# ScalarE makes a slot's coefficient ahead of its share of the mixer's work

## The reference

```
def peer_ffn(h, w_q, sub_keys, u, v):          # in chunks of 128 tokens
    q = (xc @ w_q).reshape(128, 8, 2, 128)
    s = einsum('thpd,pnd->thpn', q, sub_keys)
    sv, si = top_k(s, 16)                      # per half
    top_s, pos = top_k(sums of all 16 x 16 pairs, 16)
    idx = the experts at pos
    g = softmax(top_s)
    act = gelu(einsum('td,thkd->thk', xc, u[idx]))
    return einsum('thk,thkd->td', g * act, v[idx])
```

## Time and profile before

| | |
|---|---|
| median of 3 runs | 2242.47 us (2241.41 to 2242.71) |
| the profiled execution | 2243.3 us, span 2241.5 us |
| granted PE clock, mean | 0.979 |
| PE busy | 2026.6 us (90%) |
| DVE busy | 1587.6 us (71%) |
| ACT busy | 1111.0 us (50%) |
| POOL busy | 622.2 us (28%) |
| gather: 512 indirect DMAs | first issued at 810.5 us, last at 2213.1 us |

### The profile page before, as it was taken

The page is one execution under the profiler, slowest core; times in us unless marked ns, Lnnn a source line. Parts: engine busy times, 40 slices in busy tenths (PEclk is TensorE's granted clock), DMA queues, the critical chain, the costliest instruction groups (busy, mean ns, idle before and its releaser), DMA issues.

```text
span 2241.5 us, 28545 instructions
## 1 busy us (share of the span) xinstructions
PE 2026.6 (90%) x9926; PEld 1299.9 (58%) x9926; DVE 1587.6 (71%) x3688; ACT 1111.0 (50%) x2704; POOL 622.2 (28%) x612
## 2 busy tenths in 40 slices
PE   8899999999999988887789979998999999888876
PEld 7789999789999975432234434443444443333322
DVE  7857778768788888666676486567567656776654
ACT  5456436466534455454444475444356544444543
POOL 0000011100011024344433343344234344444442
PEclk9899999999999999999999999999999999999999
DMA  6225698726598579999999999999999999999996
GB/s 236 77 94 203 222 339 294 248 84 213 195 357 301 186 276 413 421 421 421 422 421 412 421 416 421 405 421 411 420 419 392 421 421 422 421 422 421 421 421 289
DMA packets 130773, 764.58 MB, mean 341 GB/s; under 512 B 14416, under 2 KB 16208, under 8 KB 59088
## 3 DMA queue, kind: packets, MB, share of 16 engines
q0 software_dynamic: 87552, 587.24, 64.1%
q1 hardware_dynamic: 42368, 174.15, 21.6%
q10 hardware_dynamic: 720, 1.51, 0.2%
HBM read 761.80 MB, written 1.05 MB: 340 GB/s over the span
## 4 chain that ended last, share of the span: by engine, by line
PE 52%; DMA 30%; DVE 10%; ACT 4%; issue 3%; POOL 1%; DVEq 0%; POOLq 0%; ACTq 0%
DMA arena<-experts,arena 28%; PE bank L1082 15%; PE bank L589 9%; PE bank L591 9%; PE bank L590 9%; PE bank L1118 7%; DVE arena L2664 3%; DMA alibi<-ada_w 1%; POOL arena L560 1%; DVE wlo L1969 1%; ACT arena L1696 1%; PE bank L773 1%; ACT arena L1480 1%; ACT arena L1695 1%; DMA arena<-ada_w 1%
## 5 line engine op out<-in xcount | busy, mean ns | idle before, releaser
L1082 PE MATMUL bank<-arena 128*128 128x512 f32 x2048 | 979.2, 617 | 154.3 <-ACT arena L1696 153.8
L2664 DVE CUSTOM_DVE_ANT_0 arena<-arena 128x1024 f32<-128x1024 f32 x512 | 626.1, 1224 | 444.6 <-DMA arena<-experts,arena 443.8
L560 POOL DMA_INDIRECT arena<-experts,arena x512 | 570.8, 1115 | 928.8 <-PE bank L1082 792.0
L1082 PEld LDWEIGHTS bank<-arena 128*128 128x128 f32 x2048 | 375.3, 194 | 708.9 <-issue 364.5
L1691 ACT ACTIVATE arena<-arena 128x1 f32<-128x1 f32 x512 | 103.3, 202 | 563.5 <-DVE arena L2664 561.5
L1367 ACT CAST whi<-wring 128x1024 fp32r<-128x1024 f32 x229 | 239.2, 1050 | 226.7 <-PE bank L591 221.4
L1969 DVE TENSOR_TENSOR wlo<-wring,whi 128x1024 fp32r<-128x1024 f32 x229 | 279.0, 1223 | 73.3 <-ACT whi L1367 72.6
L1696 ACT ACTIVATE arena<-tab,arena 128x128 f32<-128x128 f32 x512 | 205.6, 401 | 16.7
L549 POOL DMA_DIRECT2D arena<-ada_w x64 | 34.2, 535 | 571.0 <-DVE adaM L2016 558.0
L589 PE MATMUL bank<-hTh,whi 128*128 128x256 f32 (+1 forms) x584 | 170.5, 292 | 1.9 <-DVE wlo L1969 1.4
L591 PE MATMUL bank<-hTh,wlo 128*128 128x256 f32 (+1 forms) x584 | 165.4, 283 | 0.0
(11 more groups left out here) (403 smaller groups left out, 2897.1 us busy)
## 6 DMA issues: line engine op xcount, KB each, us to landing
wring<-w_stream SPq DMA_DIRECT2D x233, 512.0 KB, 4.3
wring<-w_stream SPq DMA_DIRECT2D x46, 1024.0 KB
arena<-ada_w POOLq DMA_DIRECT2D x64, 512.0 KB, 5.5
alibi<-ada_w POOLq DMA_DIRECT2D x32, 512.0 KB, 5.5
arena<-experts,arena POOLq DMA_INDIRECT x512
xT<-xT_in SPq DMA_DIRECT2D x2, 544.0 KB, 4.2
alibi<-alibi_in ACTq DMA_DIRECT2D x1, 1024.0 KB, 5.3
tab<-tab_in SPq DMA_DIRECT2D x1, 847.0 KB, 10.6
```

What stands on the lines that cost most here:

```text
L560: pool.indirect_dma_start(g_ring[:, r], None, experts[n // (2 * PEER_HEADS)], bass.IndirectOffsetOnAxis(idx[:, s // SLOTS % 2, s % SLOTS:s ...
L1082: last = mm(banks[2 * t + b][:, :], diag[:, r], g_ring[:, r, D + b * TILE_N:D + (b + 1) * TILE_N], start=s % SLOTS == 0, stop=s % SLOTS == ...
L2664: v.tensor_tensor_reduce(g_ring[:, r, 0:D], g_ring[:, r, 0:D], hrow[:, t], 1.0, 0.0, ALU.mult, ALU.add, act8[:, r:r + 1]).then_inc(dot_don ...
```

## The change

In ACT's loop over the slots behind the early ones (slots 0 to 59 are done in an earlier loop, without parts), the call of coefficient(s) goes from behind the parts that begin at slot s to ahead of them:

```
             beside = [None, mixer_parts(0), mixer_parts(1), last_parts(0)]
             for s in range(early, N_SLOTS):
+                coefficient(s)
                 for _ in range(parts_begun(s)):
                     next(beside[s // SLOTS])
-                coefficient(s)
             last_rows()
```

## The result

The changed kernel takes 2247.87 us (median of 20 runs, 2244.39 to 2251.88) against 2243.05 for the kernel before in the same comparison (20 runs, 2240.88 to 2245.58). The ratio is 1.0020, 95% interval 1.0014 to 1.0026: **4.8 us slower**. The forecast was 2254, 11.5 slower. The direction was right and the time lies inside the range; the size was over twice too large, and a size is what the working claimed to give. The *no change* rival had 2242 to 2247, whose upper end is nearer to the result than the forecast is. The profiled execution has a span of 2246.3 us, against 2241.5.

What follows compares the result with a forecast made beforehand. DMA at its 421 to 422 GB/s ceiling was taken as the bound, with 9.5 us of empty transfer time to regain. 2243.3 + 2.3 + 1.0 + 5 + 3 = 2254.6, less 0.83 for the median: 2254 us; range 2241 to 2265.

Steps and rivals of the forecast that it cites:

- no change: Rival: the ring covers both tiles' delays but for the copies of (a), or less; 2242 to 2247 us, chance 0.21.
- (a): copy_f at slot 3 of each mixer: PE's transposes start 2.27 us later; +2.3 us at tile 1, +1.0 at tile 0.
- (b) tile 0's pairs: Softmax pairs of tile 0's mixer: shorter operations, fuller queue, last dot 6.4 us late; +3 us of empty DMA time.
- (b) tile 1's pairs: Softmax pairs at slots 36, 40, 43, 47: Exp load comes onto the path, DVE's stream late; +5 us of empty DMA time.
- (c): Norm parts: square root later, coefficient earlier, opposing edits; oT copies later but transfers full behind them; 0 us.
- (d): Parts waiting for PE (row copy L1736): coefficient no longer behind that wait, PE has diagonals in hand; 0 us.
- The walk through the pairs: Tile 1's four pairs, step by step: joins 2.1, 4.1, 7.3 us late, fourth adds 3.7, slot 48's dot 7.6 late.
- the allowance for cover: Behind tile 1's pairs: queue covers about two late gathers; +5 us taken, against 7.6 if nothing is covered.
- Faster: Rival: PE's wait for the diagonal after the exponentials is the path, so the change gains; 2237 us, chance 0.08.
- Much slower: Rival: parts' results lie behind the slot's gather, PE keeps a slot less of the ring; 2273 us, chance 0.09.
- The forecast's own test: Forecast is wrong if DVE's new waits appear without GB/s below 402 in 1600 to 1700 and 419 in 1300 to 1400.
- The drain: Skill's 1.38 us per table switch at eight Exp loads: estimate 11 us, time near 2265; given no chance of its own.

Runs made afterwards that it cites:

- copies: Kernel before with the coefficient ahead of the part only at slot 3 of each tile (131, 259, 387): 2242.48 against 2242.44 us, ratio 0.9999.
- pairs_tile0: Kernel before with the coefficient ahead only at the four pair slots of tile 0's mixer: 2242.54 against 2242.44 us, ratio 1.0000.
- pairs_tile1: Kernel before with the coefficient ahead only at slots 36, 40, 43, 47 of tile 1's mixer: 2246.87 against 2242.44 us, ratio 1.0018.
- rest: Kernel before with the coefficient ahead on all slots but both mixers' pair slots and slot 3 of each tile: 2244.08 against 2242.44 us, ratio 1.0006.
- dot_first: Kernel before with ACT's coefficient and DVE's dot both ahead of the part at both mixers' pair slots: 2242.91 against 2243.06 us, ratio 1.0000.
- dve_long_tile1: Kernel before with 44 chained memsets on DVE ahead of slot 48 of tile 1's mixer: 2244.86 against 2243.18 us, ratio 1.0010.
- the four pieces: The change split into pairs_tile1, pairs_tile0, copies and rest, each applied alone to the kernel before; ratios 1.0018, 1.0000, 0.9999 and 1.0006.

## Why the prediction was right in direction and wrong in size

**The bound** was right. Transfers run at 421 or 422 GB/s while experts are gathered, before and after, and PE's waits for L1696 (98.3 us from 1140 to 2230 us before, 100.5 after) aren't what is paid: copies has 104.6 at no measured cost.

**The step that failed is the sum**: "2243.3 + 2.3 + 1.0 + 5 + 3". Three of its four terms, 6.3 of 11.3 us, were priced where they arise and not where they end. "DMA already runs dry there, so all of it counts" is the sentence that is wrong: what the copies lost at 1550 us came back at the pairs, up to 1720 us. The measured worth of the four terms:

- (a) both copies, forecast 3.3: PE's wait grew by 2.3 at each place as worked out, the time by 0.0 (copies, interval -2.2 to +1.8 us).
- (b) tile 0's pairs, forecast 3: the lag of 3.8 us at slot 48 came, with a dip of 2.4 us in the change, and went; 0.1 (pairs_tile0, interval -2.0 to +2.0).
- (b) tile 1's pairs, forecast 5: 4.4 (pairs_tile1), and 5.4 in the changed kernel's profile. This term was about right.
- (c), (d), forecast 0: 1.6 (rest), interval -0.7 to +3.4; not told from 0.

The reason could be read in the dips of the earlier trace rows: transfers wait there for the engines, so a shortfall ahead of a dip can be made up in it. Behind tile 1's pairs there is hardly any. For tile 0's pairs and for tile 1's copies the return stands outside the spread of the profiles; for tile 0's copies only the time says so. The prediction used this for the gain (no more than the empty time can be had) and not for the loss.

**The walk through the pairs** had the mechanism right: coefficient, Exp load, exponentials, join, and DVE's stream as what stays late (dot_first shows that the order of dot, masks and load is the cause; that a late stream alone is paid there has only dve_long_tile1's 1.7 us, 0.2 to 4.3, for it). Its lags were 2.1, 4.1 and 7.3 us at the joins and 7.6 at slot 48; measured are 1.5, 2.7, 5.1 and 4.5. The join waits for its own head's two exponentials and not for all four, 0.98 us per pair less. The +5 was right partly by luck: the allowance for cover was too large by about as much as the lag.

**The rivals.** Faster: out; the interval lies above 1. Much slower: out; the piece that holds the row copies costs 3.4 us at most. No change: two of the four pieces cost nothing and a third can't be told from it, so as a mechanism the rival was right for tile 0's pairs and for the copies, and wrong for tile 1's pairs. The forecast's own test held: DVE's new waits are there (seven, up to 3.0 us) and GB/s is lower in 1300 to 1400. But 407 against 419 is a weak sign, since the six kernels that leave tile 0 alone have 409 to 421 there, and 1600 to 1700 rose from 402 to 408; its loss came in the next window, 398 against 422. The drain that the Trainium skill counts in a table switch ("ScalarE: Activation LUTs", What ACT_TABLE_LOAD costs) shows in no row here: the exponential starts at 1682.39, 0.01 us behind the load.

## What to carry to other kernels

Price a loss at the point from which nothing gives it back. With a ring in front of a saturated DMA queue, list the dips of before, from more than one execution: here a delay with dips behind it cost nothing (tile 0's pairs, 0.1 us), and the same edit behind the last of them cost 4.4 us. When an operation is moved ahead of another on one engine, ask for each whether what it waits for, and its table load, ran in the shade of a wait before: here the coefficient came in front at no measured cost once DVE made its dot in front as well.

## What the runs showed of the hardware

In these traces a table load runs ahead of the wait of its activation, so that an engine that waits long enough has it for free. At tile 1's fourth pair in the kernel before, the Exp load was over at 1685.88 and its exponential waited for the mask until 1688.22:

```profile
1684.60 1.28 ACT L1767 ACT_TABLE_LOAD   x1
1688.22 0.51 ACT L1767 ACTIVATE arena<-arena 128x256 f32<-128x256 f32 x1 [2.34 <-DVE arena L2587]
```

At the third pair the load started at 1675.57, while DVE masked; behind the moved coefficient it started at 1681.10 with the masks done, and was on the path. Sixteen chained one-column activations on ACT take 3.70 us (0.23 each) and 44 chained one-column memsets on DVE 5.46 us (0.12 each).
